# Value-row buffers handed out by a table (eight become ten, twelve, nineteen), and the last norm's rows moved

## The reference

```
q  = layernorm(x1 @ w_q per head half)            # 8 heads, 2 halves of 128
s1, i1 = top16(q_a . keys_a);  s2, i2 = top16(q_b . keys_b)
sc, ci = top16(s1[:,None] + s2[None,:]);  idx = e1*128 + e2      # 16 experts per token and head
h  = gelu(u_tab[idx] . x1);   w = softmax(sc) * h
peer = sum over heads, experts of w * v_tab[idx]
x2 = LN(alpha*x1 + peer; ln2_g, ln2_b);   x3 = x2 + (p @ w_pe) * sigmoid(x2 @ w_pg)
```

## Time and profile before

| what | value |
|---|---|
| median of 3 runs | 2193.61 us (2182.48 to 2194.57) |
| the profiled execution, its own time | 2201.78 us |
| its span, first to last instruction | 2200.0 us |
| TensorE matmul busy | 1483.9 us (67%) |
| VectorE busy | 1192.6 us (54%) |
| GpSimd busy | 989.7 us (45%), x1052 |
| data moved | 675.81 MB, mean 307 GB/s |
| of it the gathers' queue | 545.33 MB, 149760 packets |
| mean granted TensorE clock | 0.801 |

### The profile page before, as it was taken

One profiled execution on the slowest core, in us unless ns is written; L12 is line 12 of the kernel. 1 busy time (PEld: TensorE's weight loads), 2 busy tenths in 40 slices (PEclk: granted clock), 3 DMA queues, 4 the chain that ended last, 5 costly groups with the idle time before them and its releaser, 6 DMA issues.

```text
span 2200.0 us, 19738 instructions
## 1 busy us (share of the span) xinstructions
PE 1483.9 (67%) x6744; PEld 922.0 (42%) x6744; DVE 1192.6 (54%) x3046; ACT 372.5 (17%) x718; POOL 989.7 (45%) x1052
## 2 busy tenths in 40 slices
PE   9999985788778688688785874463533335663455
PEld 7888874664544355456553442130300001220113
DVE  1111025766676565575667555666688676665421
ACT  2312101132321111231101111111111110111000
POOL 0000002346554355554455555656455666655651
PEclk9999997999878699888897897576755665576777
DMA  7344434799999898999998989989799999998992
GB/s 260 118 151 153 154 134 155 268 351 412 357 385 344 336 364 350 369 362 338 360 351 317 343 341 381 384 311 369 271 341 323 365 358 351 346 333 310 357 319 96
DMA packets 188260, 675.81 MB, mean 307 GB/s; under 512 B 36313, under 2 KB 38489, under 8 KB 174338
## 3 DMA queue, kind: packets, MB, share of 16 engines
q0 software_dynamic: 149760, 545.33, 66.1%
q1 hardware_dynamic: 38402, 129.23, 16.1%
HBM read 667.07 MB, written 7.41 MB: 307 GB/s over the span
## 4 chain that ended last, share of the span: by engine, by line
PE 40%; DVE 22%; issue 13%; DMA 10%; POOL 6%; another core or an unknown queue 6%; ACT 1%; SPq 0%; DVEq 0%; POOLq 0%; PEldq 0%; ACTq 0%
PE PJ L1279 14%; DVE at L1074 9%; PE PJ L1178 8%; PE Y L1327 6%; PE PJ L1164 4%; DMA at<-in_u_tab,idx 4%; DMA at<-in_v_tab,idxV 4%; POOL at L589 3%; POOL at L583 3%; PE PJ L1185 2%; DMA at<-in_w_q 1%; DVE at L1002 1%; PE PJ L1239 1%; DVE inds L1001 1%
## 5 line engine op out<-in xcount | busy, mean ns | idle before, releaser
L583 POOL DMA_INDIRECT at<-in_u_tab,idx x512 | 487.6, 952 | 744.0 <-DVEq L1058 347.5
L1074 DVE CUSTOM_DVE_ANT_0 at<-at,XD 128x1024 f32<-128x1024 f32 x512 | 614.1, 1216 | 137.0 <-DMA at<-in_u_tab,idx 101.1
L589 POOL DMA_INDIRECT at<-in_v_tab,idxV x512 | 485.5, 948 | 400.8 <-PE Y L1327 186.0
L1327 PE MATMUL Y<-at,at 128*32 128x512 f32 x2048 | 358.8, 815 | 297.1 <-DMA at<-in_v_tab,idxV 218.1
L1279 PE MATMUL PJ<-at,at 128*128 128x256 f32 (+1 forms) x1792 | 421.9, 396 | 4.0 <-issue 2.4
L1279 PEld LDWEIGHTS PJ<-at,at 128*128 128x128 f32 x1792 | 348.3, 197 | 86.5 <-issue 25.7
L1327 PEld LDWEIGHTS Y<-at,at 128*32 128x32 f32 x2048 | 73.5, 133 | 494.4 <-issue 478.5
L1178 PE MATMUL PJ<-at,at 128*128 128x256 f32 (+2 forms) x960 | 240.3, 411 | 37.6 <-DMA at<-in_w_q 24.9
L1178 PEld LDWEIGHTS PJ<-at,at 128*128 128x128 f32 (+2 forms) x960 | 179.2, 190 | 97.6 <-DMA at<-in_w_q 27.2
L1293 PE MATMUL R<-ident,at 128*128 128x128 f32 x68 | 21.0, 406 | 209.3 <-DVE at L1022 165.8
L1164 PE MATMUL PJ<-at,at 128*128 128x256 f32 (+1 forms) x640 | 145.5, 386 | 0.6 <-issue 0.6
(11 more groups left out here) (197 smaller groups left out, 1380.5 us busy)
## 6 DMA issues: line engine op xcount, KB each, us to landing
at<-in_w_blk SPq DMA_DIRECT2D x72, 1024.0 KB
at<-in_w_q SPq DMA_DIRECT2D x16, 1024.0 KB
at<-in_w_o SPq DMA_DIRECT2D x8, 1024.0 KB
at<-in_u_tab,idx POOLq DMA_INDIRECT x512
at<-in_v_tab,idxV POOLq DMA_INDIRECT x512
at<-in_state SPq DMA_DIRECT2D x4, 1024.0 KB
out_st_s<-at SPq DMA_DIRECT2D x4, 1024.0 KB
at<-in_w_pg SPq DMA_DIRECT2D x2, 2048.0 KB
```

What stands on the lines that cost most here:

```text
L583: pool.indirect_dma_start(ubuf[m % UB], None, u_tab, bass.IndirectOffsetOnAxis(rows_of, 0)).then_inc(u_in[m % UB], 16)
L589: pool.indirect_dma_start(vbuf[m % VB], None, v_tab, bass.IndirectOffsetOnAxis(rows_of, 0)).then_inc(v_in[m % VB], 16)
L1074: v.tensor_tensor_reduce(out=t, in0=t, in1=XD[:, :], scale=1.0, scalar=0.0, op0=ALU.mult, op1=ALU.add, accum_out=hraw[:, n % 2, k:k + 1]). ...
L1327: last = mm(Y[32 * c:32 * c + 32, s, :], wpadV[d // PAIR % 2][:, g, :], vbuf[m % VB][:, 512 * s:512 * s + 512], start=False, stop=final)
```

## The change

It does four things.

1. **Buffers by table.** `places` walks the gathers in order with a list of free slots and writes down for each its slot, how often the slot was used before, and which gather held it last. v gets ten buffers, from v gather 224 (`V_LATE`, GpSimd step n = 15) two more, and from v gather 492 (`V_END`, 28 gathers before the last) also the seven u buffers, whose last dots are awaited. u gets a seventh buffer from u gather 256 (`U_LATE`, the same step). The order in which gathers are issued stays.
2. **Room.** The room of the mixers' constants and state (`wsT`, `Sst`, `gkl`, `wgk`, `gl`, `bsrow`) gives the two late v buffers and the late u buffer; GpSimd waits once, at n = 15, for the second half's last `bra` job and for the store of the state.
3. **Last norm's rows.** `ln2g`, `ln2b` are now the same room as `lna_g`, `lna_b`. SyncE loads them no longer at the start but behind the last block of `w_q`, when all norms `x1` are done (`x1_ok`). The 2,048 words freed are the first two new v buffers. `qS` moves to another room.
4. **Norm of tile 0.** Since its rows come later, the norm of tile 0's result moves from position (9, 1 and 3) to (16, 9 and 11). The copy of `Y` becomes a plan entry of its own, `y`, and stays at k = 1 for each tile.

```diff
+ITERS = NT * PH
+UB, VB = 6, 10
+LATE, END = 15, ITERS - 1
+X2_OF_FIRST = 2 * PH
...
-            if n > PH and n % PH == 1 and k in (1, 3):
+            if n > PH and n % PH == 1 and k == 1:
+                out.append(("y", n // PH - 1))
+            if n > 2 * PH and n % PH == 1 and k in (1, 3):
                 out.append(("x2", n // PH - 1, k // 2))
+            if n == X2_OF_FIRST and k in (9, 11):
+                out.append(("x2", 0, k // 2 - 4))
...
+def places(first, total, more):
+    free, out, uses, holder = list(range(first)), [], {}, {}
+    for m in range(total):
+        free = more.get(m, []) + free
+        slot = free.pop(0)
+        out.append((slot, uses.get(slot, 0), holder.get(slot)))
+        uses[slot], holder[slot] = uses.get(slot, 0) + 1, m
+        free.append(slot)
+    return out
+U_LATE, V_LATE, V_END = u_number(LATE + 1, 0), v_number(LATE - 1, 0), v_number(END - 1, 4)
+U_PLACE = places(UB, u_number(ITERS - 1, TOPK - 1) + 1, {U_LATE: [UB]})
+U_LAST = sorted((m, slot) for slot, m in {p[0]: m for m, p in enumerate(U_PLACE)}.items())
+V_PLACE = places(VB, v_number(ITERS - 1, TOPK - 1) + 1,
+                 {V_LATE: [VB, VB + 1], V_END: [VB + 2 + slot for _, slot in U_LAST]})
...
-        qS = at(O_LNA, 2, 256)
-        ln2g, ln2b = take(D), take(D)
+        ln2g, ln2b = lna_g, lna_b
+        O_WS = place[0]
...
+        qS = at(O_L + 1392, 2, 256)
+        vbuf += [at(O_WS + D * i, D) for i in range(2)]
+        ubuf.append(at(O_WS + 2 * D, D))
+        vbuf += ubuf
...
-            sp.dma_start(ln2g, ln2_g.partition_broadcast(128)).then_inc(ln2_in, 16)
-            sp.dma_start(ln2b, ln2_b.partition_broadcast(128)).then_inc(ln2_in, 16)
...
                     if e == ("job", 1, "wq", PH - 1, NT):
+                        sp.wait_ge(x1_ok, NT + 1)
+                        sp.dma_start(ln2g, ln2_g.partition_broadcast(128)).then_inc(ln2_in, 16)
+                        sp.dma_start(ln2b, ln2_b.partition_broadcast(128)).then_inc(ln2_in, 16)
                         sp.wait_ge(pj_done, JOB[e] + 1)
...
             def gather_v(m, rows_of):
-                if m >= VB:
-                    pool.wait_ge(v_used, m - VB + 1)
-                pool.indirect_dma_start(vbuf[m % VB], None, v_tab, bass.IndirectOffsetOnAxis(rows_of, 0)).then_inc(
-                    v_in[m % VB], 16)
+                slot, _, held_by = V_PLACE[m]
+                if held_by is not None:
+                    pool.wait_ge(v_used, held_by + 1)
+                elif slot >= VB + 2:
+                    pool.wait_ge(u_used, dict((s, u) for u, s in U_LAST)[slot - VB - 2] + 1)
+                pool.indirect_dma_start(vbuf[slot], None, v_tab, bass.IndirectOffsetOnAxis(rows_of, 0)).then_inc(
+                    v_in[slot], 16)
...
+                if n == LATE:
+                    pool.wait_ge(pj_done, JOB["job", 1, "bra", 3, 1] + 1)
+                    pool.wait_ge(stp_out, 16)
...
-                        v.wait_ge(y_done, j + 1)
-                        v.tensor_copy(t.rearrange("p (a b) -> p a b", a=2), Y[:, :, :]).then_inc(y_read, 1)
                         v.wait_ge(y_read, j + 1)
...
+                elif what == "y":
+                    j = args[0]
+                    v.wait_ge(y_done, j + 1)
+                    v.tensor_copy(x1[:, j, :].rearrange("p (a b) -> p a b", a=2), Y[:, :, :]).then_inc(y_read, 1)
```

More of the change, by code:

```diff
@@ L37 @@
 AHEAD = 4
-UB, VB = 6, 8
+ITERS = NT * PH
+UB, VB = 6, 10
+LATE, END = 15, ITERS - 1
+X2_OF_FIRST = 2 * PH
 PAIR = 2 * TOPK
-ITERS = NT * PH
 SAMPLE_ROUTES_AT = 21
@@ L223, in plan @@
             out.append(("gelu", n + 1))
-    out += [("x2", NT - 1, part) for part in range(2)] + rest(NT - 1)
+    out += [("y", NT - 1)] + [("x2", NT - 1, part) for part in range(2)] + rest(NT - 1)
     return out
@@ L438, in decoder_step @@
             "varr_ok", "sdr_ok", "qn_ok", "qt_done", "qt_ok", "s_done", "sc_ok", "exp_in", "exp_ok", "route_ok", "idxv_ok"))
-        u_in = [sem(f"u_in{i}") for i in range(UB)]
-        v_in = [sem(f"v_in{i}") for i in range(VB)]
+        u_in = [sem(f"u_in{i}") for i in range(len(ubuf))]
+        v_in = [sem(f"v_in{i}") for i in range(len(vbuf))]
         u_used, v_used, h_ok, g_ok, w_ok, wpv_ok, ap_ok, y_done, y_read = (sem(n) for n in (
@@ L579, in gather_u @@
             def gather_u(m, rows_of):
[L581 to L584, removed]
-            def gather_v(m, rows_of):
-                if m >= VB:
-                    pool.wait_ge(v_used, m - VB + 1)
-                pool.indirect_dma_start(vbuf[m % VB], None, v_tab, bass.IndirectOffsetOnAxis(rows_of, 0)).then_inc(
-                    v_in[m % VB], 16)
+                slot, _, held_by = U_PLACE[m]
+                if held_by is not None:
+                    pool.wait_ge(u_used, held_by + 1)
+                pool.indirect_dma_start(ubuf[slot], None, u_tab, bass.IndirectOffsetOnAxis(rows_of, 0)).then_inc(
+                    u_in[slot], 16)
+            def gather_v(m, rows_of):
+                slot, _, held_by = V_PLACE[m]
+                if held_by is not None:
+                    pool.wait_ge(v_used, held_by + 1)
[3 more added lines that the diff above has]
+                    v_in[slot], 16)
             for n in range(-1, ITERS + 1):
@@ L956, in combine @@
                     m = u_sample(i)
-                    v.wait_ge(u_in[m % UB], 16 * (m // UB + 1))
-                    t = ubuf[m % UB][:, 512 * c:512 * c + 512]
+                    slot, before, _ = U_PLACE[m]
+                    v.wait_ge(u_in[slot], 16 * (before + 1))
+                    t = ubuf[slot][:, 512 * c:512 * c + 512]
                     v.tensor_tensor_reduce(out=t, in0=t, in1=src, scale=1.0, scalar=0.0, op0=ALU.mult, op1=ALU.add,
@@ L1071, in dot @@
                     link(v.tensor_copy(XD[:, :], x1[:, n // PH, :]))
-                v.wait_ge(u_in[m % UB], 16 * (m // UB + 1))
-                t = ubuf[m % UB]
+                slot, before, _ = U_PLACE[m]
+                v.wait_ge(u_in[slot], 16 * (before + 1))
+                t = ubuf[slot]
                 v.tensor_tensor_reduce(out=t, in0=t, in1=XD[:, :], scale=1.0, scalar=0.0, op0=ALU.mult,
@@ L1267, in job @@
                         m = v_sample(b)
-                        pe.wait_ge(v_in[m % VB], 16 * (m // VB + 1))
-                        last = mm(out[0:S, :], wpad[:, b, :], vbuf[m % VB][:, 512 * i:512 * i + 512], start=b % 4 == 0,
+                        slot, before, _ = V_PLACE[m]
+                        pe.wait_ge(v_in[slot], 16 * (before + 1))
+                        last = mm(out[0:S, :], wpad[:, b, :], vbuf[slot][:, 512 * i:512 * i + 512], start=b % 4 == 0,
                                   stop=b % 4 == 3)
@@ L1319, in sums @@
                     pe.wait_ge(wpv_ok, d // PAIR + 1)
-                four = [v_number(n, k + i) for i in range(4)]
-                for m in four:
-                    pe.wait_ge(v_in[m % VB], 16 * (m // VB + 1))
+                four = [V_PLACE[v_number(n, k + i)][0] for i in range(4)]
+                for m in range(v_number(n, k), v_number(n, k) + 4):
+                    slot, before, _ = V_PLACE[m]
+                    pe.wait_ge(v_in[slot], 16 * (before + 1))
                 for s in range(2):
-                    for i, m in enumerate(four):
+                    for i, slot in enumerate(four):
                         g = tokens_of((d + i) % PAIR)
@@ L1327, in sums @@
                         last = mm(Y[32 * c:32 * c + 32, s, :], wpadV[d // PAIR % 2][:, g, :],
-                                  vbuf[m % VB][:, 512 * s:512 * s + 512], start=False, stop=final)
+                                  vbuf[slot][:, 512 * s:512 * s + 512], start=False, stop=final)
                         if s == 1:
@@ L1331, in sums @@
                 if final:
-                    pe.wait_ge(v_used, four[3] + 1)
+                    pe.wait_ge(v_used, v_number(n, k + 3) + 1)
                     pe.sem_inc(y_done, 1)
```

## The result

The changed kernel was slower: 2230.18 us median (4 runs, 2216.70 to 2242.79) against 2190.74 (4 runs, 2182.48 to 2194.57), ratio 1.0184 with an interval of 1.0116 to 1.0253. The forecast, 2135 with 2085 to 2186, missed in size and in sign. Its profiled run took 2227.92 us, span 2226.1, against 2201.78 and 2200.0.

The account below looks back on a forecast made before the run. The prediction took GpSimd's queue, issue plus waits for u and v buffers, to bound the late part. Late part -40, middle -10, tail -12, moved rows +3 gave -59 us: 2135 against the median 2193.61, range 2085 to 2186.

Parts of the forecast that it names:

- the v buffers' middle part: Middle part: two more v buffers remove most v waits; -10 us at the end, bounds 0 and 34.
- The u ring takes the wait over: Rival: GpSimd's v waits turn into u waits, leaving only the tail's gain and moved rows: -9, 2185 us; chance 0.17.
- the 21%: Middle part: share of waiting where GpSimd is later than the dots, 34.0 / 159.9, making 130.1 us worth 28 for VectorE.
- The lower bound of 0: Middle part: smallest effect allowed for the two more v buffers, no gain; the upper bound was 34 us.
- The late part: Late part: nearly all 86.0 us of v waits go, 47% of it counting; -40 us, bounds 0 and 86.
- under 20, less than 50: Late part, expected signs: GpSimd's v waits under 20 us, its u waits grown by less than 50.
- My 47%: Late part: share of waiting where GpSimd is later than the dots, 67.0 / 142.5, making 86.0 us worth 40.
- The tail: Last 32 v gathers issue without waits, leaving the transfer, faster at 391 GB/s; -12 us, bounds 5 and 14.
- The moved rows: Last norm's rows, loaded behind w_q, take DMA time where gathers want it; +3 us, bounds 0 and 15.
- The ceiling of 358 GB/s: Rival: 358 GB/s is all that holds over hundreds of us, limiting the gain to -46, 2148 us; chance 0.08.
- Weight blocks behind more gathers: Rival, middle part: two more gathers ahead of w_o and w_q blocks cost 32 us; +23, 2217 us; chance 0.10.

Follow-up runs that it names:

- e3: Kernel before with only the last norm's rows and tile 0's norm moved, eight v and six u buffers throughout: 2202.72 us, ratio 0.9998, slower place.
- e4: Kernel before with rows and norm moved, plus nineteen v buffers from gather 492: 2196.03 us, ratio 0.9965, slower place.
- e18: Same kernel as e4, run again in the slower place: 2185.83 us, ratio 0.9984 to the kernel before.
- e12: Same kernel as e3, each gather also waiting until the seventh before it has landed: ratio 1.0015 to the kernel before, faster place.
- e8: Same kernel as e3, each gather also waiting until the fifth before it has landed: ratio 1.0105 to the kernel before, faster place.
- e1: Changed kernel with eight instead of ten v buffers until gather 224, then twelve and nineteen: 2199.12 us, ratio 0.9993 to the kernel before, slower place.
- e16: Same kernel as e1, run in the faster place: ratio 0.9816 to the kernel before.
- e2: Changed kernel with ten v and six u buffers all along, none added later: 2235.98 us, ratio 1.0146 to the kernel before, slower place.
- e15: Same kernel as e2, run in the faster place: ratio 0.9866 to the kernel before.
- e7: Same kernel as e2, each gather also waiting until the fifth before it has landed: ratio 0.9991 to the kernel before, faster place.
- e6: Changed kernel, each gather also waiting until the seventh before it has landed: ratio 0.9854 to the kernel before, faster place.
- e11: Same kernel as e6, run again in the faster place: ratio 0.9833 to the kernel before.
- e14: Same kernel as e6, run again in the faster place: ratio 0.9835 to the kernel before.
- e17: Same kernel as e6, run in the slower place: 2245.27 us, ratio 1.0228 to the kernel before.
- e5: Changed kernel, each gather also waiting until the fifth before it has landed: ratio 0.9932 to the kernel before, faster place.
- e10: Changed kernel, unaltered, run in the faster place: 2056.72 us, ratio 0.9795 to the kernel before.
- e9: Kernel before, unaltered, run in the faster place for its trace: ratio 0.9998.
- e13: Changed kernel, unaltered, run again in the faster place: ratio 0.9817 to the kernel before.

## Why the prediction was wrong

Two tables carry it. First the ratios by kernel and place:

| v buffers: middle, late, end | slower place | faster place |
|---|---|---|
| 8, 8, 8 (e3) | 0.9998 | not run |
| 8, 8, 19 (e4, e18) | 0.9965, 0.9984 | not run |
| 8, 8, 8, cap 7 (e12) | not run | 1.0015 |
| 8, 8, 8, cap 5 (e8) | not run | 1.0105 |
| 8, 12, 19 (e1, e16) | 0.9993 | 0.9816 |
| 10, 10, 10 (e2, e15) | 1.0146 | 0.9866 |
| 10, 10, 10, cap 5 (e7) | not run | 0.9991 |
| 10, 12, 19 (after) | 1.0184 | 0.9795, 0.9817 |
| 10, 12, 19, cap 7 (e6, e11, e14; e17) | 1.0228 | 0.9854, 0.9833, 0.9835 |
| 10, 12, 19, cap 5 (e5) | not run | 0.9932 |

Then where the time goes, from the start of dots in VectorE's order of time (after less before, in us; in the faster place e10 less e9). Dot 288, taken as the border of the middle and the late part, before and after in the slower place:

```profile
1389.07 1.22 DVE L1074 CUSTOM_DVE_ANT_0 at<-at,XD 128x1024 f32<-128x1024 f32 x1 [0.19 <-issue]
```
```profile
1437.04 1.22 DVE L1110 CUSTOM_DVE_ANT_0 at<-at,XD 128x1024 f32<-128x1024 f32 x1 [0.41 <-DMA at<-in_u_tab,idx]
```


| piece | slower | faster | forecast |
|---|---|---|---|
| up to dot 0 (355.5 to 358.1; 362.2 to 355.6) | +2.6 | -6.6 | |
| dot 0 to dot 288 (1389.1 to 1437.0; 1353.7 to 1347.0) | +45.4 | -0.1 | -10 |
| dot 288 to the last (2107.9 to 2147.2; 2004.4 to 1977.1) | -8.7 | -20.6 | -40 |
| the last dot to the end (2200.0 to 2226.1; 2101.2 to 2059.9) | -13.1 | -14.0 | -12 |
| sum | +26.1 | -41.3 | -62, with the +3 of the moved rows -59 |

The first row is no effect of the change: over fourteen profiles, of both places and most of the kernels, dot 0 starts between 354.7 and 362.2 us, in no order by kernel.

**The step that failed is the v buffers' middle part.** I took 10 us of gain between bounds of 0 and 34; it is 0 in the faster place and 45 us of loss in the slower. The eight profiles of the slower place bear out that this is the buffers and not chance: from dot 0 to dot 288 the five with eight v buffers there (before, e1, e3, e4, e18) take 1027 to 1048 us, the three with ten (after, e2, e17) 1070 to 1079. For the first half of the miss the profile is plain. GpSimd's waits in e9, then in e10, 480 to 1330:

```profile
POOL at L583 <- DVE hraw L1074: 136.4, 81, 6.6
POOL at L589 <- PE Y L1327: 121.0, 36, 10.9
```
```profile
POOL at L613 <- DVE hraw L1110: 252.7, 110, 10.4
...
POOL at L622 <- PE Y L1369: 19.1, 18, 4.5
```

102 us of v waits went and 116 of u waits came: the first rival, "The u ring takes the wait over", is what the middle part did. GpSimd serves both rings in one order, so it stops at whichever is full. I had seen that u was the next limit and still counted the 21% as won.

**The lower bound of 0 was the graver error.** It said that a buffer more can't cost. In the slower place it did, and the profile of before had a sign in two rows that I took for ordinary waits: VectorE's copy released by "remote" seven times for 53.7 us, and the v gather's 28.1. I put both down to waits that the change would shrink. They are late releases: these two became 41.8 and 10.2 us, but ScalarE's in the middle part grew, and after the change the row's part of the chain was 13% for 6%. The engines behind TensorE start late, TensorE waits for routing (98.4 for 66.2 us), and the ring slows in step. That late releases go with ten v buffers is seen in all eight profiles of that place: ScalarE's waits that end in "remote", 480 to 1330, add up to 91 to 116 us with eight and to 170 to 174 with ten. By what mechanism is open. That they cause the 45 us is argued from these rows, not shown by itself, since no kernel removed them in that place; nor is it known what makes TensorE stand still there.

**The late part** had the right sign and was forecast too large: twice what it gave in the faster place, more than four times in the slower, where the -8.7 is one pair of profiles and e1 and e17 with the same late buffers (e17 with the cap besides) show no gain (725.2 and 733.1 us for 718.8 before). In the faster place the gain is steady: from dot 288 to the last, 630 to 632 us with the late buffers (e10, e13, e16), 650.7 in e9 and 649.8 with ten all along (e15). There, GpSimd's waits from 1330 to 2100 in e9, then e10:

```profile
POOL at L589 <- PE Y L1327: 66.8, 38, 6.2
POOL at L583 <- DVE hraw L1074: 32.4, 37, 3.0
POOL at L589 <- PEq L1284: 16.8, 2, 11.7
```
```profile
POOL at L613 <- DVE hraw L1110: 62.4, 64, 5.7
...
POOL at L622 <- PEq L1325: 9.5, 2, 6.6
POOL at L622 <- PE Y L1369: 5.9, 14, 1.9
```

v waits 83.6 to 15.4, u waits up by 30, as the forecast wanted (under 20, less than 50). The dots' waits for u tiles in that stretch went from 72.4 to 47.4, 25 us, near the 20.6 gained. My 47% counted every wait of a dot as GpSimd being late; 47.4 us of such waits are left although the v waits are nearly gone. That these are gathers issued in time and still in transfer is likely, but not shown.

**The tail** came out at its number in both places, 13.1 and 14.0 for 12. Nineteen buffers are not needed for it: e15 with ten has its last dot at 1997.5 and its end at 2080.3, 82.8 us, the same as e10's 82.8.

**The moved rows**, +3, cost nothing that can be measured (e3).

**The ceiling of 358 GB/s**, the second rival, fell. Stretch 1330 to 2000 in e9 and in e10:

```profile
1330.00:2000.00 670.00, 326.50 (x1466) 119.52 (x1466) 483.66 (x1254) 103.28 (x183) 447.46 (x472) 0.69 0.98 376
```
```profile
1330.00:2000.00 670.00, 334.41 (x1522) 123.25 (x1526) 487.53 (x1261) 105.88 (x190) 465.26 (x489) 0.68 1.01 388
```

670 us were held at 388 GB/s, by one core running alone. The Trainium skill (DMA: Bandwidth & Descriptors, Specifications) gives about 358 for each core of the two that share a stack of HBM; over this stretch the measurement is above it, and decides. The row also suggests what bounds the late part now in the faster place: the DMA share is 1.01, so more buffers there have little left to win (single slices of 51 us of e10's page reach 409 GB/s in it). No run tried more.

**Weight blocks behind more gathers**, the rival that ended slower, was not the reason for the slower result: TensorE's waits for w_q and w_o went from 22.4 to 25.7 us, and in the faster place from 14.3 + 6.5 = 20.8 to 17.5 + 6.5 = 24.0. The one long wait, 15.4 us, follows a late release: SyncE's issue of that block at 1273.36 came with ScalarE's copy that "remote" released at the same moment, 9.9 us after the matmuls' end by the profile. The Trainium skill (same page, Queues, rings and completion order) has an engine alternate between its queues packet by packet; waits of 3 us more in 850 do not speak against it, and are no test of it.

**Which version to keep.** In the faster place the changed kernel and e16 are equal and best. In the slower one e16's twin e1 is level with before while the changed kernel loses 1.8%. Eight v buffers until gather 224 and the change's table from there has the whole gain in the faster place and no loss in the slower. No version here beats both kernels in both places.

## What to carry to other kernels

When one queue serves two rings in a fixed order, a buffer more in one ring moves the wait to the other unless the other has slack in the same stretch; count the gain from the consumers' own waits, not from the queue's. Don't put zero as a bound on harm for buffering that lets an engine run further ahead: read every wait that ends by nothing the profile can name, and ask what the change does if that wait doesn't shrink. And before an explanation is built on experiments from two groups of runs, put the unchanged kernel and the suspected cure side by side in one group, and look at the base's own time.

## What the runs showed that I had not expected

The same program took 2098 to 2103 us in three groups of runs and 2191 to 2202 in the others, 4 to 5% more, with nearly the same granted clock in the front part (0.93 and 0.94 to 480 us) and the same 0.94 us for a gather's issue. The difference lies where gathers run: from dot 0 to dot 288 the kernel before takes 42 us more in the slower place, from there to the last dot 68. There the engines behind TensorE are at times released late, 6 to 11 us after its matmuls end by the profile at the three spots above, and TensorE and ScalarE stand still with nothing named that they wait for. Late releases and these pauses may have one cause; no run separates them. Whether the chip or what goes on around it makes the place is not known: e1 to e4 (slower) and e9 to e12 (faster) carry the same chip number, 5, so if that number means one chip, the chip alone does not. A change of buffering can be worth -2% in one and +1.8% in the other, each with an interval that leaves out 1.
